# One kernel on one NeuronCore: the order of the query tiles in the prompt attention

## The chip, the cores and the metric

The kernel is one layer of a hybrid model, written in Bass for Trainium2. It runs as one program on one core of one chip. The metric is device time in microseconds (us), the median of several executions; the profile shows one execution of its own.

## The reference

A layer takes a prompt of 1024 tokens and a decode batch of 8 sequences with 4 tokens each. Half of the mixer is a gated linear recurrence (HGRN2), the other half is sparse attention with 8 query heads in 2 key-value groups (width 64), followed by an output projection and a convolutional feed-forward. The change touches the attention of the prompt alone. Its three branches, cut to the core:

```
o_cmp = softmax over compressed blocks of 16 tokens (63 of them), masked by position
o_slc = softmax over selected blocks of 64, at most 16: with 1024 prompt tokens all causal ones
o_win = softmax over the last 512 tokens
o = g[0] * o_cmp + g[1] * o_slc + g[2] * o_win      # g: sigmoid gates per token and head
```

With 1024 tokens there are only 16 blocks of 64, so that the selected branch is plain causal attention: query tile `qt` (128 queries) reads `qt + 1` key blocks of 128. The window branch reads at most 5 of them.

## The kernel before, in words

Six stages follow one another, with a barrier between them. `prompt_attention` is the fourth of them. It works through a list `units` written at L517 to L534: for each of the two key-value groups g one compressed unit C (all 8 query tiles at once), and then for every query tile qt one selected unit (SLC, S0 to S7 below) and one window unit (WND, W0 to W7). That makes 34 units. A unit Sq reads q + 1 key blocks, a unit Wq reads q + 1 of them up to 5.

Each unit has two halves of work:
- The **front**: for its 4 heads, TensorE computes scores (`scores`, L847 to L872) into one of two PSUM buffers `ps`, VectorE takes the row maximum (L781), ScalarE the exponential with its row sum (L694). A unit of up to 256 keys handles all 4 heads in one fill of a PSUM buffer, one of up to 512 keys two heads a fill, and a longer one needs 4 fills. A fill waits until the exponentials of the fill before last are done (L850 to L851). After the front VectorE computes four coefficients a row (L794, L795) and GpSimd scales the unit's probabilities by them (L651; L657 for unit C).
- The **back**, in groups of one key block each: TensorE transposes the scaled probabilities of 4 heads (`turn`, L890), ScalarE copies their high part (L708), VectorE forms the low part (L803), and TensorE multiplies both with the values (L910, L911) into the one accumulator `acc`. Even tiles have one more group in the window unit, for the compressed probabilities of two tiles (L704, L906, L907); odd ones use them again without a transpose (L914, L915). So the tiles must come in pairs 2k, 2k + 1.

After the last group of a window unit the tile's output leaves `acc` (L715 on ScalarE, L808 and L815 on VectorE), and SyncE stores it (L627).

All engines follow one list of steps. In step i, from -3 to 34, the back of unit i is interleaved with the front of unit i + 3:

```
    def merged(i):
        back = units[i].groups if 0 <= i < NU else 0
        front = units[i + AHEAD].fills if i + AHEAD < NU else 0
```

Steps -3 to 0 hold fronts alone (the fill of the pipeline), steps 31 to 34 backs alone (its drain). Steps 14 to 17 are the passage from group 0 to group 1, with unit C of group 1, whose front is long on TensorE. Every engine takes its instructions strictly in this order. In steps 1 to 3 ScalarE and VectorE also split the values and queries of group 1 (`second_high`, `second_low`; L676, L752, L680, L757).

SyncE has one queue: the stores of tile outputs in their order, between them the weights of the next stage (`w5a` at L623, `w5b` at L632), and from L633 on the first rows of the next stage (`o_front`, `x_front`).

Of the kernel before, what the change touches and what calls it, by code (L numbers as in the profile page):

```python
# [501 lines left out]
def prompt_attention(nc, io, keep, scratch, consts_sb):  # L502
# [3 lines left out]
    NQ = T // P  # L506
    NBK = NCP - 1
    CB = NCP
    CMP, SLC, WND = 0, 1, 2
# [4 lines left out]

    units = []
    n_fills = n_heads = n_groups = n_dense = 0
    for g in range(NG):  # L517
        for kind, qt in [(CMP, 0)] + [(kind, qt) for qt in range(NQ) for kind in (SLC, WND)]:
            u = Unit()
            u.n, u.g, u.kind, u.qt = len(units), g, kind, qt  # L520
            u.k0 = max(0, qt - 4) if kind == WND else 0
            u.blocks = [] if kind == CMP else list(range(u.k0, qt + 1))
            u.w = NQ * CB if kind == CMP else len(u.blocks) * P
            u.per = 4 if u.w <= 256 else 2 if u.w <= 512 else 1
            u.fills = R // u.per
            u.fill0, u.head0, u.group0, u.dense = n_fills, n_heads, n_groups, n_dense
            u.pair = kind == WND and qt % 2 == 0
            u.groups = len(u.blocks) + u.pair
            n_fills += u.fills
            n_groups += u.groups  # L530
            if kind != CMP:
                n_heads += R
                n_dense += 1
            units.append(u)  # L534
# [4 lines left out]
    pv_of_group, pv_before, n_pv = {}, {}, 0  # L539
# [19 lines left out]
    with ExitStack() as ctx:  # L559
# [30 lines left out]
        t_ready, h_ready, l_ready, pv_ready = (sem(n) for n in ("t_ready", "h_ready", "l_ready", "pv_ready"))  # L590
        half_ready, lower_ready, oT_ready = sem("half_ready"), sem("lower_ready"), sem("oT_ready")
        oT_out = [sem("oT_out0"), sem("oT_out1")]
# [19 lines left out]
        @block.sync  # L612
        def _(sp):
            for h in range(R):
                if h >= 2:
                    sp.wait_ge(qL_ready, h - 1)
                for d in range(2):
                    sp.dma_start(qs[h % 2][64 * d:64 * d + 64, :], scratch["q_T"][:, R + h, 0:T]).then_inc(q_in[h % 2], 16)
            sp.wait_ge(consts_sb["soft"]["p7_o_out"], 256)
            sp.wait_ge(kT_ready, 4)  # L620
            sp.wait_ge(vL_ready, 2)
            for k in range(4):
                sp.dma_start(keep["w5a"][:, k], io["w_out"][0, k * P:(k + 1) * P, :]).then_inc(consts_sb["soft"]["p5_w_in0"], 16)  # L623
            for a in range(NG * NQ):
                g, qt = a // NQ, a % NQ
                sp.wait_ge(oT_ready, 2 * (a + 1))
                sp.dma_start(scratch["o_T"][256 * g:256 * g + 256, qt * P:qt * P + P].rearrange("(k p) t -> p k t", p=P),  # L627
                             oT[a % 2][:]).then_inc(oT_out[a % 2], 16)
                if a == NQ:
                    sp.wait_ge(s_ready, units[NU // 2].fill0)  # L630
                    for k in range(4):
                        sp.dma_start(keep["w5b"][:, k], io["w_out"][0, (4 + k) * P:(5 + k) * P, :]).then_inc(consts_sb["soft"]["p5_w_in1"], 16)  # L632
                if a == NQ + 4:  # L633
                    sp.wait_ge(qL_ready, R)
                    for t in range(2):
                        sp.wait_ge(oT_out[t], 16 * (NQ // 2 + 1))
                        rows = slice(t * P, t * P + P)
                        done = consts_sb["soft"][f"p5_front_in{t}"]
                        sp.dma_start(keep["o_front"][:, t, 0:HGW], scratch["o_mix"][rows, 0:HGW]).then_inc(done, 16)
                        sp.dma_start(keep["o_front"][:, t, HGW:D].rearrange("p (k c) -> p k c", k=4),  # L640
                                     scratch["o_T"][:, rows].rearrange("(k p) c -> p k c", p=P)).then_inc(done, 16)
                        sp.dma_start(keep["x_front"][:, t], io["x_prompt"][0, rows, :]).then_inc(done, 16)
            for i in range(2):
                sp.wait_ge(oT_out[i], 16 * (NG * NQ // 2))
# [22 lines left out]
        def _(act):  # L667
# [29 lines left out]
            def high_of(u, k):  # L697
                G = u.group0 + k
                act.wait_ge(t_ready, G + 1)
                src = pt[G % 3][:].rearrange("p b c -> p (b c)")  # L700
                if u.pair and k == u.groups - 1:
                    if u.qt + u.g > 0:
                        act.wait_ge(pv_ready, pv_before[u.n - 2 if u.qt else u.n - 3])
                    nc.scalar.copy(PcH[:], src).then_inc(h_ready, 1)  # L704
                else:
                    if G >= 3:
                        act.wait_ge(pv_ready, pv_of_group[G - 3])
                    nc.scalar.copy(PTH[:, G % 3, :], src).then_inc(h_ready, 1)  # L708

            def upper_half(u):  # L710
                a = u.g * NQ + u.qt
                act.wait_ge(pv_ready, pv_before[u.n])
                if a >= 1:
                    act.wait_ge(oT_ready, 2 * a)
                nc.scalar.copy(half[:], acc[64:128, :]).then_inc(half_ready, 1)  # L715
# [25 lines left out]
        def _(dve):  # L741
# [61 lines left out]
                nc.vector.tensor_tensor(lo, src, hi.bitcast(F32), ALU.subtract).then_inc(l_ready, 1)  # L803

            def both_halves(u):
                a = u.g * NQ + u.qt
                dve.wait_ge(pv_ready, pv_before[u.n])
                nc.vector.tensor_copy(lower[:], acc[0:64, :]).then_inc(lower_ready, 1)  # L808
                dve.wait_ge(half_ready, a + 1)
                dve.wait_ge(lower_ready, a + 1)  # L810
                if a >= 2:
                    dve.wait_ge(oT_out[a % 2], 16 * (a // 2))
                for odd in range(2):
                    at = lambda x: x.rearrange("p (k o c) -> p k o c", k=2, o=2)[:, :, odd]
                    nc.vector.tensor_tensor(oT[a % 2][64 * odd:64 * odd + 64], at(lower[:]), at(half[:]), ALU.add).then_inc(oT_ready, 1)  # L815
# [22 lines left out]
        def _(pe):  # L838
# [53 lines left out]

            def values(u, k):
                G = u.group0 + k
                a = u.g * NQ + u.qt
                out = acc[:]
                pe.wait_ge(l_ready, G + 1)
                if u.kind == SLC and k == 0:
# [19 lines left out]
            for i in range(-AHEAD, NU + 1):  # L918
# [5 lines left out]
                for what, k in order:  # L924
# [5 lines left out]
                    else:  # L930
                        u = units[i + AHEAD]
# [2130 lines left out]
```

## Time and profile before

| | us |
|---|---|
| median of 3 runs | 2410.34 (2406.26 to 2414.07) |
| the profiled execution, its own time | 2406.49 |
| span of the profile | 2404.70 |
| from the first scores of the prompt attention (1171.28) to the store of its last tile (1472.16) | 300.88 |

The span is what the trace covers, from the first to the last instruction; the execution's own time is 1.79 us longer. All times below are from the start of the span.

### The profile page before, as it was taken

Reading aid. Unit: us, or ns where it says so; the run is one execution under the profiler, and the core shown is the slowest. Engines: PE = TensorE matmul, PEld = TensorE weight load, DVE = VectorE, ACT = ScalarE, POOL = GpSimd, SP = SyncE. Lnnn points to the kernel's source line nnn. Section 1 sums busy time; section 2 is a strip of 40 time slices with the busy share of each in tenths; the row PEclk is TensorE's granted clock in tenths of the full one; section 3 lists DMA queues with packets and bytes.
Section 4 is the critical chain, followed back from the end, with each engine's and each line's share of the span. In section 5 each row is a group of like instructions: output and inputs, shape, how many; then the busy total and the mean of one; then the engine's idle time right before and its main releaser. Section 6 shows DMA issues by size and latency. Waiting matters only on the chain. (4 is left out here: it accounts for less than half of the span.)

```text
span 2404.7 us, 39963 instructions
## 1 busy us (share of the span) xinstructions
PE 2256.3 (94%) x15806; PEld 2032.7 (85%) x15806; DVE 1307.0 (54%) x2975; ACT 945.3 (39%) x1910; POOL 513.0 (21%) x874
## 2 busy tenths in 40 slices
PE   6999999999999999869889898989999999999998
PEld 5999987877778777648767676869999999999998
DVE  5124137767767768743487786543333334355556
ACT  4114124555545544422275675212222222144444
POOL 0001004333324332200187683100000000011110
PEclk9999999999999999879699999989999999999999
DMA  4215726645446544297120112311111111122223
GB/s 122 68 53 188 279 100 214 219 161 182 167 151 217 172 155 133 52 284 229 36 62 5 44 43 72 109 52 49 44 44 52 44 44 44 52 84 80 81 72 119
DMA packets 213557, 263.10 MB, mean 109 GB/s; under 512 B 32658, under 2 KB 180370, under 8 KB 204018
## 3 DMA queue, kind: packets, MB, share of 16 engines
q1 hardware_dynamic: 195240, 159.71, 22.0%
q0 software_dynamic: 18160, 101.27, 12.1%
q8 instruction: 102, 1.67, 0.3%
q14 instruction: 55, 0.45, 0.1%
HBM read 202.76 MB, written 65.05 MB: 111 GB/s over the span
## 5 line engine op out<-in xcount | busy, mean ns | idle before, releaser
L1549 PE MATMUL f<-hH,wH 128*128 128x352 f32 x1056 | 341.4, 323 | 5.2 <-DVE wL L1422 5.2
L1549 PE MATMUL f<-hL,wH 128*128 128x352 f32 x1056 | 339.1, 321 | 0.0
L1549 PE MATMUL f<-hH,wL 128*128 128x352 f32 x1056 | 338.7, 321 | 0.0
L2527 ACT CAST a_XTH<-cpt 64x256 fp32r<-64x256 f32 (+1 forms) x576 | 200.9, 349 | 146.4 <-PE cpt L2734 135.8
L2643 DVE TENSOR_TENSOR a_XTL<-cpt,a_XTH 64x256 fp32r<-64x256 f32 (+1 forms) x576 | 230.3, 400 | 29.8 <-ACT a_XTH L2527 21.5
L1564 PE MATMUL f<-wdH,aH 128*128 128x256 f32 (+1 forms) x792 | 222.1, 285 | 8.7 <-DVE aL L1475 4.8
L1564 PE MATMUL f<-wdL,aH 128*128 128x256 f32 (+1 forms) x792 | 220.1, 284 | 0.0
L2749 PE MATMUL cph<-a_XTH,w1H 128*128 128x512 f32 x512 | 216.4, 423 | 0.0
L2749 PE MATMUL cph<-a_XTH,w1L 128*128 128x512 f32 x512 | 204.1, 399 | 0.0
L2749 PE MATMUL cph<-a_XTL,w1H 128*128 128x512 f32 x512 | 204.1, 399 | 0.0
L1549 PEld LDWEIGHTS f<-hH,wH 128*128 128x128 f32 x1056 | 198.6, 188 | 5.3 <-DVE wL L1422 5.3
L1564 PE MATMUL f<-wdH,aL 128*128 128x256 f32 x704 | 200.3, 285 | 0.0
L1549 PEld LDWEIGHTS f<-hL,wH 128*128 128x128 f32 x1056 | 198.9, 188 | 0.0
L1549 PEld LDWEIGHTS f<-hH,wL 128*128 128x128 f32 x1056 | 198.5, 188 | 0.0
L1422 DVE TENSOR_TENSOR wL<-raw,wH 128x1024 fp32r<-128x1024 f32 x44 | 53.8, 1225 | 225.1 <-ACT wH L1325 222.6
L1475 DVE TENSOR_TENSOR aL<-a_aT,aH 128x1408 fp32r<-128x1408 f32 x64 | 104.0, 1624 | 103.8 <-ACT aH L1363 103.5
L1564 PEld LDWEIGHTS f<-wdH,aH 128*128 128x128 f32 (+1 forms) x792 | 148.2, 187 | 11.0 <-DVE aL L1475 5.5
L1363 ACT CAST aH<-a_aT 128x1408 fp32r<-128x1408 f32 (+1 forms) x72 | 91.4, 1269 | 147.3 <-PE f L1564 147.3
L1564 PEld LDWEIGHTS f<-wdL,aH 128*128 128x128 f32 (+1 forms) x792 | 145.9, 184 | 0.0
L1564 PEld LDWEIGHTS f<-wdH,aL 128*128 128x128 f32 x704 | 136.3, 194 | 0.0
L486 PE MATMUL pj<-wH,xL 128*128 128x256 f32 (+2 forms) x464 | 130.9, 282 | 0.0
L486 PE MATMUL pj<-wH,xH 128*128 128x256 f32 (+2 forms) x464 | 130.8, 282 | 0.0
(486 smaller groups left out, 5358.4 us busy)
## 6 DMA issues: line engine op xcount, KB each, us to landing
raw<-in_w_in POOLq DMA_DIRECT2D x12, 1024.0 KB, 6.1
a_V<-v_s SPq DMA_DIRECT2D x6, 2048.0 KB, 12.1
v_s<-X SPq DMA_DIRECT2D x22, 512.0 KB, 6.2
raw<-in_w_gate SPq DMA_DIRECT2D x22, 512.0 KB, 3.9
raw<-in_w_val SPq DMA_DIRECT2D x22, 512.0 KB, 3.9
wraw<-in_w_down SPq DMA_DIRECT2D x44, 256.0 KB, 4.0
z_tok<-stage SPq DMA_DIRECT2D x48, 128.0 KB, 5.0
a_akq<-hq SPq DMA_DIRECT2D x32, 192.0 KB, 5.3
```

The lines of the kernel that those rows point to most:

```text
L486: last = nc.tensor.matmul(bank[u % 8][0:r, 0:nw], xp[:, k, a * P:a * P + r], wp[:, j % 2, k, 0:nw], **flags)
L1363: nc.scalar.copy(aH[:, h, :, 0:r], aT[:, NFH * h:NFH * h + NFH, t * P:t * P + r]).then_inc(aH_ready, 1)
L1422: nc.vector.tensor_tensor(wL[:, a], raw[:, a], wH[:, a].bitcast(F32), ALU.subtract).then_inc(wL_ready, 1)
L1475: nc.vector.tensor_tensor(dst, aT[:, NFH * h:NFH * h + NFH, t * P:t * P + r], aH[:, h, :, 0:r].bitcast(F32), ALU.subtract).then_inc(aL_rea ...
L1549: last = nc.tensor.matmul(bank[3 * a + n][:, 0:w], wp[:, a, k, :], hp[:, k, c0:c0 + w], start=(k + part == 0), stop=(k == KD - 1 and part ...
L1564: last = nc.tensor.matmul(bank[t % 3][0:rows, 0:QW], ap[:, h, j, 0:rows], wp[:, f, :], start=first, stop=final)
L2527: nc.scalar.copy(turned(XTH, u, s, k, g, a), split(bank(at, k)[:], u, k, g, a)).then_inc(h_ready, 1)
L2643: last = nc.vector.tensor_tensor(turned(XTL, u, s, k, g, a), split(bank(at, k)[:], u, k, g, a), hi.bitcast(F32), ALU.subtract)
L2749: last = nc.tensor.matmul(out[:, :, 0:n], w[:, s, k, q, m * P:(m + 1) * P], x[:, s % 2, k, :, q:q + n], **flags)
```

## The change

The query tiles of both groups are taken in the order 6 7 0 1 4 5 2 3 in place of 0 to 7. Buffers, semaphores and accumulations that counted by the tile number now count by its place in the order (`u.at`). SyncE stores the tiles in the new order, and starts the loads of `o_front` and `x_front`, which need tiles 0 and 1 of both groups, after the fourteenth of the 16 stores, one store later than before.

```diff
+    ORDER = [6, 7, 0, 1, 4, 5, 2, 3]
     for g in range(NG):
-        for kind, qt in [(CMP, 0)] + [(kind, qt) for qt in range(NQ) for kind in (SLC, WND)]:
+        for kind, qt in [(CMP, 0)] + [(kind, qt) for qt in ORDER for kind in (SLC, WND)]:
             u = Unit()
+            u.at = 0 if kind == CMP else ORDER.index(qt)
...
-                g, qt = a // NQ, a % NQ
+                g, qt = a // NQ, ORDER[a % NQ]
...
-                if a == NQ + 4:
+                if a == NQ + 5:
                     sp.wait_ge(qL_ready, R)
                     for t in range(2):
-                        sp.wait_ge(oT_out[t], 16 * (NQ // 2 + 1))
+                        sp.wait_ge(oT_out[t], 16 * (NQ // 2 + 2))
...
-                    if u.qt + u.g > 0:
-                        act.wait_ge(pv_ready, pv_before[u.n - 2 if u.qt else u.n - 3])
+                    if u.at + u.g > 0:
+                        act.wait_ge(pv_ready, pv_before[u.n - 2 if u.at else u.n - 3])
...
-                a = u.g * NQ + u.qt
+                a = u.g * NQ + u.at
```

(The last replacement stands at three places: `upper_half`, `both_halves` and `values`.)

What this does to the engines is seen first on GpSimd, from the scaling of unit C of group 0 on, for the first four tiles. Before, rows of `a_Prs` (selected units) and `a_Prw` (window units) widen from 128 columns:

```order
L657 TENSOR_TENSOR a_Pc<-a_Pc,a_cfc 128x2048
L651 TENSOR_SCALAR a_Prs<-a_Prs,a_cf 128x128 x4
L651 TENSOR_SCALAR a_Prw<-a_Prw,a_cf 128x128 x4
L651 TENSOR_SCALAR a_Prs<-a_Prs,a_cf 128x256 x4
L651 TENSOR_SCALAR a_Prw<-a_Prw,a_cf 128x256 x4
L651 TENSOR_SCALAR a_Prs<-a_Prs,a_cf 128x384 x4
L651 TENSOR_SCALAR a_Prw<-a_Prw,a_cf 128x384 x4
```

Now, at the same place (line numbers in the changed kernel are two higher):

```order
L659 TENSOR_TENSOR a_Pc<-a_Pc,a_cfc 128x2048
L653 TENSOR_SCALAR a_Prs<-a_Prs,a_cf 128x896 x4
L653 TENSOR_SCALAR a_Prw<-a_Prw,a_cf 128x640 x4
L653 TENSOR_SCALAR a_Prs<-a_Prs,a_cf 128x1024 x4
L653 TENSOR_SCALAR a_Prw<-a_Prw,a_cf 128x640 x4
L653 TENSOR_SCALAR a_Prs<-a_Prs,a_cf 128x128 x4
L653 TENSOR_SCALAR a_Prw<-a_Prw,a_cf 128x128 x4
L653 TENSOR_SCALAR a_Prs<-a_Prs,a_cf 128x256 x4
```

The four widest units of a group stand first, the four narrowest right behind them. VectorE at the fill of the pipeline (steps -2 to 0), from the coefficients of unit C on, before:

```order
L781 TENSOR_REDUCE a_nm<-s 128x4
L794 RECIPROCAL a_den<-a_den 128x4
L795 TENSOR_TENSOR a_cf<-a_den,gates 128x4
L781 TENSOR_REDUCE a_nm<-s 128x4
L794 RECIPROCAL a_den<-a_den 128x4
L795 TENSOR_TENSOR a_cf<-a_den,gates 128x4
L781 TENSOR_REDUCE a_nm<-s 128x2
```

and now:

```order
L783 TENSOR_REDUCE a_nm<-s 128x1 x4
L796 RECIPROCAL a_den<-a_den 128x4
L797 TENSOR_TENSOR a_cf<-a_den,gates 128x4
L783 TENSOR_REDUCE a_nm<-s 128x1 x4
L796 RECIPROCAL a_den<-a_den 128x4
L797 TENSOR_TENSOR a_cf<-a_den,gates 128x4
L783 TENSOR_REDUCE a_nm<-s 128x1 x4
```

Each front that took one fill and one maximum over all four heads now takes four fills and four maxima, before the first transpose of the back can follow. At the drain, VectorE's last rows before:

```order
L803 TENSOR_TENSOR a_PTL<-pt,a_PTH 128x512 x2
L808 COPY a_lower<-acc 64x512
L815 TENSOR_TENSOR a_oT<-a_lower,a_half 64x256 x2
L803 TENSOR_TENSOR a_PTL<-pt,a_PTH 128x512 x11
L808 COPY a_lower<-acc 64x512
L815 TENSOR_TENSOR a_oT<-a_lower,a_half 64x256 x2
```

and now:

```order
L805 TENSOR_TENSOR a_PTL<-pt,a_PTH 128x512 x2
L810 COPY a_lower<-acc 64x512
L817 TENSOR_TENSOR a_oT<-a_lower,a_half 64x256 x2
L805 TENSOR_TENSOR a_PTL<-pt,a_PTH 128x512 x6
L810 COPY a_lower<-acc 64x512
L817 TENSOR_TENSOR a_oT<-a_lower,a_half 64x256 x2
```

The last tile (S3, W3) has 8 groups where it had 13 (S7, W7); with W2 in place of W6 in step 31 the drain has 12 groups in place of 19. No instruction of the stage is added or removed.

## Rows read from the trace of the kernel before

**Rows 1.** the page of the profile, its first line.

```profile
span 2404.7 us, 39963 instructions
```

**Rows 2.** stretches of the prompt attention, all engines; columns in the first line.

```profile
core 0: us, PE busy (x) PEld busy (x) DVE busy (x) ACT busy (x) POOL busy (x), PEclk, DMA share, GB/s
1171.28:1186.64 15.36, 15.36 (x70) 14.97 (x69) 4.01 (x5) 1.78 (x3) 0.00 (x0) 0.50 0.14 35
1186.64:1196.04 9.40, 8.29 (x38) 7.81 (x38) 8.46 (x11) 3.96 (x17) 2.11 (x1) 0.50 0.00 0
1196.04:1305.12 109.08, 94.37 (x545) 79.46 (x546) 92.80 (x144) 78.27 (x173) 94.59 (x61) 0.95 0.12 37
1305.12:1346.88 41.76, 35.05 (x225) 30.07 (x224) 27.41 (x41) 17.61 (x42) 15.15 (x10) 0.92 0.02 4
1346.88:1448.33 101.45, 90.20 (x545) 76.31 (x545) 87.08 (x140) 73.55 (x167) 90.47 (x56) 0.98 0.15 51
1448.33:1472.14 23.81, 20.22 (x121) 15.55 (x119) 17.92 (x30) 13.29 (x24) 9.20 (x5) 1.00 0.02 6
```

**Rows 3.** timeline of the stage's end; start, duration, engine, line, operation, idle before.

```profile
1470.06 0.40 PE L915 MATMUL acc<-a_PcL,VC 128*128 128x512 f32 x1
...
1472.16 0.36 SPq L627 DMA_DIRECT2D o_T<-a_oT  x1
```

**Rows 4.** timeline of TensorE: one fill (1406.27), two transposes a group apart.

```profile
1406.27 0.40 PE L866 MATMUL s<-a_KTb,a_Qb 128*128 128x512 f32 x1
...
1407.19 0.60 PE L890 MATMUL pt<-ident,a_Prw 128*128 128x128 f32 x4
...
1408.09 0.60 PE L890 MATMUL pt<-ident,a_Prw 128*128 128x128 f32 x4
```

**Rows 5.** groups by shape, VectorE, 1220 to 1472: count, busy, mean ns, idle, releaser.

```profile
L803 DVE TENSOR_TENSOR a_PTL<-pt,a_PTH 128x512 fp32r<-128x512 f32 x128 | 87.5, 688 | 28.9 <-ACT a_PTH L708 26.8
L781 DVE TENSOR_REDUCE a_nm<-s 128x1 f32<-128x640 f32 x40 | 32.8, 820 | 1.3 <-PE s L871 1.0
...
L808 DVE COPY a_lower<-acc 64x512 f32<-64x512 f32 x15 | 10.1, 674 | 1.3 <-PE acc L915 1.3
...
L781 DVE TENSOR_REDUCE a_nm<-s 128x1 f32<-128x896 f32 x8 | 8.7, 1083 | 0.2
...
L787 DVE TENSOR_REDUCE a_denc<-a_Pc 128x32 f32<-128x2048 f32 x1 | 2.3, 2274 | 0.0
```

**Rows 6.** groups by shape, ScalarE, 1220 to 1472.

```profile
L694 ACT ACTIVATE a_Prw<-s,a_nm 128x640 f32<-128x640 f32 x32 | 25.5, 798 | 21.7 <-DVE a_nm L781 21.6
L694 ACT ACTIVATION_READ_ACCUMULATOR a_Prs<-s,a_nm 128x1 f32 x52 | 10.3, 198 | 0.0
...
L694 ACT ACTIVATE a_Prs<-s,a_nm 128x896 f32<-128x896 f32 x8 | 8.1, 1010 | 3.8 <-DVE a_nm L781 3.6
```

**Rows 7.** list of waits, 1171 to 1472: us in total, times, longest.

```profile
ACT a_Prw L694 <- DVE a_nm L781: 31.9, 19, 2.8
DVE a_PTL L803 <- ACT a_PTH L708: 27.0, 51, 1.2
...
PE acc L910 <- DVE a_lower L808: 11.1, 12, 3.5
```

**Rows 8.** timeline of GpSimd: scaling of C, S6, S7 in group 0.

```profile
1193.93 3.62 POOL L657 TENSOR_TENSOR a_Pc<-a_Pc,a_cfc 128x2048 f32<-128x2048 f32 x1 [161.54 <-DVE a_cfc L790]
...
1275.21 10.04 POOL L651 TENSOR_SCALAR a_Prs<-a_Prs,a_cf 128x896 f32<-128x896 f32 x4 [2.11 <-DVE a_cf L795]
...
1295.39 11.43 POOL L651 TENSOR_SCALAR a_Prs<-a_Prs,a_cf 128x1024 f32<-128x1024 f32 x4 [1.32 <-DVE a_cf L795]
```

**Rows 9.** timeline of VectorE: the two additions of a tile's output.

```profile
1229.26 0.87 DVE L815 TENSOR_TENSOR a_oT<-a_lower,a_half 64x256 f32<-64x256 f32 x2
...
1329.52 2.55 DVE L815 TENSOR_TENSOR a_oT<-a_lower,a_half 64x256 f32<-64x256 f32 x2
```

**Rows 10.** DMA issues, 1380 to 1500: count, KB each, median us to landing.

```profile
x_front<-in_x_prompt SPq DMA_DIRECT2D x2, 512.0 KB, 5.6
```

More of the change, by code:

```diff
@@ L805, in both_halves @@
             def both_halves(u):
-                a = u.g * NQ + u.qt
+                a = u.g * NQ + u.at
                 dve.wait_ge(pv_ready, pv_before[u.n])
@@ L894, in values @@
                 G = u.group0 + k
-                a = u.g * NQ + u.qt
+                a = u.g * NQ + u.at
                 out = acc[:]
```

## Prediction

> **What bounds the kernel now.** I read the page first [rows 1]: the span is 2404.70 us, and the profiled execution took 2406.49. Then I cut the prompt attention into stretches [rows 2]. Their borders are the first TensorE instruction of a step, found by counting TensorE's rows in the timeline against the program's order: steps -2 to 0 are 1186.64 to 1196.04, steps 1 to 13 end at 1305.12, 14 to 17 at 1346.88, 18 to 30 at 1448.33, and the drain ends with the store of the last tile at 1472.16 [rows 3]. The reader is to see two things there. First, no engine is full: in steps 1 to 13 TensorE is busy for 94.4 of 109.1 us, VectorE for 92.8, GpSimd for 94.6; in 18 to 30 for 90.2, 87.1 and 90.5 of 101.5. Second, the three are alike, so whichever has most to do in a step sets that step, and the rest is handover. The list of waits says the same [rows 7]: ScalarE waits 31.9 us for maxima, VectorE 27.0 for high parts, TensorE 11.1 for the accumulator to be emptied. So the order can change only how long the pipeline fills and drains, and how evenly the steps load the engines.
>
> **Term 1, the fill: +18 us.** Before, steps -2 to 0 take 9.4 us [rows 2], because S0, W0 and S1 need one fill each. Now S6, W6 and S7 need four each, twelve in all. A fill of S6 takes TensorE 0.92 us at the full clock (1406.27 to 1407.19) [rows 4], up to twice that while the granted clock is 0.50, as it is in this stretch [rows 2]; then VectorE takes 1.08 [rows 5], ScalarE 1.01 and 0.20 [rows 6], and three handovers cost about 0.1 to 0.2 each. With two PSUM buffers two fills share one such chain of about 3.9 us (TensorE's part taken between the two clocks), so one costs 1.95; for W6 (VectorE 0.82, ScalarE 0.80) it is 1.55. VectorE also has unit C's coefficients in between: 2.3 for the sum [rows 5] and about 0.8 for three short ones. I walked it: S6's first maximum ends near 1190.8, C's coefficients near 1194.1, S6's last exponential near 1200.7, W6's near 1207.7, S7's third at 1213.9. Step 1 begins with a fill that needs this last one: 1214 in place of 1196, which is +18. From below: GpSimd starts S6 when the coefficients are there, 1200 at best, and needs 10.04 us [rows 8], and no transpose of S6 comes before 1210: +14. From above: twelve fills at 2.4 us (half clock throughout) and 3.1 for C: 1219, +23.
>
> A rule weighed here: the Trainium skill, "TensorE: Matmul & The Clock Gate", Part 1, says that the reduced clock is the default and sustained activity of the array releases it. This trace agrees as far as it goes: the clock is 0.50 over C's narrow matmuls and the small fills behind them, and 0.95 in the mean of steps 1 to 13. By that rule the wider matmuls of S6 and W6 would bring the full clock some microseconds earlier; the sum would have +15 here in place of +18.
>
> **Term 2, the two long stretches: -8 us.** I added up each step's work for both orders. VectorE: 0.69 us a group (L803), for a maximum 0.16 us and 1.03 ns a column (the line through 0.82 at 640 and 1.08 at 896) [rows 5], 0.35 for the two short operations on a unit's coefficients, 1.95 for a tile's output (0.67 for L808 [rows 5], and 1.28 for L815 between 0.87 and 2.55 [rows 9]). TensorE: 0.90 a group (1407.19 to 1408.09), 0.92 a fill of 896 columns, others in proportion [rows 4]. Step 13 before, for one, holds 7 groups of S6, four maxima of W7, coefficients and an output: VectorE 4.8 + 3.3 + 0.35 + 1.95 = 10.4, TensorE 9.8. The larger load, summed over the steps, is 98.7 for steps 1 to 13 and 92.6 for 18 to 30; the trace has 109.08 and 101.45 [rows 2], so a step costs 1.10 times its larger load. In the new order the sums are 95.0 and 91.3: times 1.10, 204.9 in place of 210.5, -5.6. They fall because work left these steps: the fronts of S6, W6 and S7 stand in the fill and the passage, and more of the backs, seven groups, come into them. VectorE's loads alone go from 187.7 to 177.5; if it paced everything, at 1.12 as before, that would be -11.4. Small steps behind long ones let the queues even out in part, so I take -8, between the two. The small tiles in the middle are not free: W7's last group is multiplied only when TensorE reaches W0's first transposes, VectorE holds its next maximum until that output is out, and a fill of S4 waits some 3 us; this is in the 1.10.
>
> **Term 3, the passage between the groups: +2 us.** Steps 14 to 17 take 41.76 us [rows 2]. They lose 7 groups of S7, W7 and W6 in the sum (19 before, 12 now), and gain the twelve fills of S6, W6 and S7 for three: TensorE's load goes from 28.4 to 30.3 and VectorE's from 29.3 to 34.3. Both engines have room there (35.1 and 27.4 busy of 41.8), and a walk like that of term 1 gave 41.8 again. I take TensorE's difference, +2; the bounds are 0 and +5.
>
> **Term 4, the drain: -6.3 us.** Steps 31 to 34 hold 12 groups for 19, with nothing beside them: seven by 0.90 [rows 4]. At the 1.1 us that a group costs with its waits it is 7.7, and 5 if the last tile's output, now behind shorter steps, is waited for.
>
> **What costs nothing.** The loads of `o_front` and `x_front` start one store later, and so nearer the end: after the output of tile 5, near step 30, some 16 us before the last store. Six issues of half a microsecond and 5.6 us to land [rows 10] make 9; if that cover were gone, the last store would wait for them by up to 9 us. GpSimd needs 10.0, 7.5, 11.4 and 7.5 us for S6, W6, S7 and W7 [rows 8] (W at the same rate a column), one behind the other until about 1238; TensorE wants W7 some 30 us after step 1 starts, 1244, so it is not late, with 6 us to spare. VectorE and ScalarE's split of group 1's values and queries, 6 us on VectorE, now falls on full steps; its load is in the sums.
>
> **The sum.** 18 - 8 + 2 - 6.3 = +5.7. On the profiled execution's own 2406.49 that is 2412.2. The median of the runs shown is 2410.34, 3.85 above this execution, so the forecast for the median is 2416.0. A measurement of this kernel can tell about 0.3% (7.2 us) from no change: below 2403.1 is faster, above 2417.6 slower.
>
> **The rivals.**
> - Evening out pays for the long fill. VectorE paces all (-11.4), the passage shortens by 2 because the fills of S6 cover C's long front, the drain gives 7.7, the fill costs only 14: -7.1, and 2403.2; with a passage 3 shorter still, 2400. For it: VectorE's ratio of measured to load is nearly the same in both stretches, 1.126 and 1.118. Against it: TensorE has the larger load in half of the new steps. Chance 0.18.
> - The tile outputs get slower. L815 took 0.87 us a pair at 1229.26 and 2.55 at 1329.52 [rows 9]; the second is while GpSimd scales, the first too, but with shorter instructions. If the wide units up front bring ten of the 16 pairs from 0.9 to 2.5, VectorE has 16 us more, half of it on the path: 2424. It decides from 1.6 us on, where the forecast crosses 2417.6. Against it: GpSimd's busy time is the same 211.5 us (the sum of its column [rows 2]) in both orders. Chance 0.16. The Trainium skill, "SBUF — State Buffer", section "SBUF: two separate sides", states a mechanism: a VectorE operation with two SBUF inputs and a GpSimd operation exclude each other on a shared port pair, for a whole instruction. The two rows of L815 agree with it; by it a pair could wait as long as one scaling of 1024 columns.
> - The order does not matter: what is saved in the middle and the drain is the fill and no more, 2410. Chance 0.08.
> - The forecast, 2410 to 2422 by the bounds of its terms: chance 0.58, of it 0.34 below 2417.6, 0.23 above and 0.01 below 2403.1.
>
> **How the numbers follow.** Faster: 0.17 of the first rival and 0.01: 0.18. Same: 0.34, 0.01, 0.03 and 0.08: 0.46. Slower: 0.23 and 0.13: 0.36. The range reaches from 2403 (the first rival's sum) to 2425 (the second's), with a tenth outside on either side.
>
> **What would show it.** TensorE's first group (step 1) near 1214; steps 1 to 13 in 103 to 106 us and 18 to 30 in 97 to 101; the passage in 42 to 45; from the last maximum to the last store 17 to 18 us for 24. The page's VectorE and GpSimd busy times within 5 us of before. The prediction is wrong if the granted clock is full right behind C and the fill takes 14 or less, if the long stretches fall by 12 or more together, if L815's pairs take 2 us or more, or if TensorE waits for GpSimd at the first transposes of S6 or S7.

## The result and the profile after

The new order is slower. Its median is 2438.86 us (2432.53 to 2439.96) against 2410.52 for the kernel before in the same comparison, a ratio of 1.0113 with a 95% interval of 1.0095 to 1.0132. The forecast was 2416, with a range to 2425.

The page of the changed kernel and its stretches of the prompt attention, cut at the same steps as [rows 2] (the columns are the same; unit C's front, steps -2 to 0, 1 to 13, 14 to 17, 18 to 30, 31 to the last store):

```profile
span 2436.6 us, 39964 instructions
...
1170.73:1183.01 12.28, 12.28 (x71) 12.01 (x69) 4.00 (x5) 1.78 (x3) 0.00 (x0) 0.64 0.19 43
1183.01:1211.00 27.99, 21.54 (x66) 16.42 (x66) 18.25 (x23) 12.44 (x23) 17.30 (x7) 0.61 0.00 0
1211.00:1324.92 113.92, 94.74 (x558) 79.91 (x559) 83.18 (x139) 73.76 (x172) 81.44 (x54) 0.94 0.11 34
1324.92:1377.94 53.02, 47.60 (x212) 41.46 (x210) 32.49 (x46) 21.93 (x42) 27.07 (x14) 0.69 0.02 6
1377.94:1484.86 106.92, 93.47 (x559) 79.37 (x560) 78.91 (x136) 69.59 (x167) 78.31 (x53) 0.95 0.08 28
1484.86:1503.85 18.99, 13.92 (x79) 10.15 (x77) 14.15 (x23) 9.34 (x18) 8.98 (x6) 1.00 0.39 125
```

Set against [rows 2], the differences are: unit C -3.1, fill +18.6, steps 1 to 13 +4.8, passage +11.3, steps 18 to 30 +5.5, drain -4.8: +32.3, and the span grew by 31.9. The fill and the drain came as forecast. Two lines did not. The long stretches grew, though VectorE has 9.6 and 8.2 us less to do in them (83.18 for 92.80, 78.91 for 87.08); TensorE's busy time did not fall with it (94.74 for 94.37, 93.47 for 90.20). And the passage runs at a granted clock of 0.69 in place of 0.92.

The list of waits, 1171 to 1504 (us in total, times, longest), answers to [rows 7]:

```profile
ACT a_PTH L710 <- PE pt L892: 60.8, 55, 7.7
...
DVE a_PTL L805 <- ACT a_PTH L710: 43.1, 60, 1.6
...
DVE a_nm L783 <- PE s L873: 26.2, 29, 2.3
...
PE acc L912 <- DVE a_lower L810: 19.4, 10, 4.2
```

and one line of the kernel before, 1171 to 1472, beside them:

```profile
DVE a_nm L781 <- PE s L871: 5.0, 8, 2.7
```

VectorE waits more for TensorE's scores (26.2 us for 5.0, the long fill included) and for ScalarE's high parts (43.1 for 27.0), and TensorE's wait for an emptied accumulator has gone from 11.1 to 19.4 us. In the two long stretches alone TensorE waits 15.2 us for the accumulator where it was 6.3, and 7.3 for low parts where it was 1.5; for probabilities it waits 11.0 where it was 18.5. These waits and its longer busy time (+3.6) add up to 10.8 us, and the two stretches grew by 10.3. The tile outputs, the second rival of the prediction, are the group L817 by shape, over the whole of the stage (count, busy, mean ns):

```profile
L817 DVE TENSOR_TENSOR a_oT<-a_lower,a_half 64x256 f32<-64x256 f32 x32 | 15.7, 490 | 2.0
```

A pair takes 0.98 us in the mean; the forecast of that rival needed 1.6 or more for ten of the pairs. It is not the cause.

### The profile page after: what moved, and what is told of

Its sections match the earlier page's. It is cut to its first block and busy times, and to the rows that moved or that the text cites. A ratio compares the mean times of both kernels' runs of the same rounds, so it can differ in the third digit from the quotient of the medians.

```text
span 2436.6 us, 39964 instructions
## 1 busy us (share of the span) xinstructions
PE 2272.9 (93%) x15806; PEld 2043.8 (84%) x15806; DVE 1303.9 (54%) x2975; ACT 946.8 (39%) x1910; POOL 512.5 (21%) x874
```

## The experiments

In all of them the order of tiles is the one line `ORDER = [6, 7, 0, 1, 4, 5, 2, 3]`, written for each group apart where they differ. With it moves the place of the loads of `o_front` and `x_front`: behind the thirteenth store in the kernel before, the fourteenth in the new order and wherever group 1 starts with 6 7 0 1, the twelfth where tiles 0 and 1 come first in group 1, and the last one in 6 7 4 5 0 1 2 3. Times are medians with the ratio to the kernel before, measured beside it; stretches come from one profile each. "C, fill, 1-13, passage, 18-30, drain" are in us, the drain to TensorE's last matmul (22.1 before, 17.3 after). Nothing ahead of the stage is changed, yet it began anywhere from 1170.4 to 1181.5 us in these profiles; so stretches are compared, and not spans. The stretches of one kernel vary too: two more profiles of the new order, below, gave 116.6 and 113.4 us for steps 1 to 13 and 106.9 and 106.1 for 18 to 30.

| kernel | ratio (95%) | C | fill | 1-13 | passage | 18-30 | drain |
|---|---|---|---|---|---|---|---|
| before | 1 | 15.4 | 9.4 | 109.1 | 41.8 | 101.5 | 22.1 |
| new order | 1.0113 (1.0095-1.0132) | 12.3 | 28.0 | 113.9 | 53.0 | 106.9 | 17.3 |
| group 1 alone new | 1.0041 (1.0028-1.0053) | 9.3 | 9.4 | 109.2 | 53.7 | 105.6 | 17.1 |
| group 0 alone new | 1.0093 (1.0066-1.0120) | 15.4 | 27.8 | 115.7 | 36.3 | 101.4 | 22.1 |
| 6 7 4 5 0 1 2 3 | 1.0083 (1.0062-1.0105) | 12.3 | 28.0 | 109.1 | 42.8 | 101.3 | 16.9 |
| 0 1 6 7 2 3 4 5 | 1.0059 (1.0038-1.0081) | 12.3 | 9.4 | 118.7 | 42.0 | 109.4 | 19.3 |
| 0 1 2 3 6 7 4 5 | 0.9989 (0.9979-0.9998) | 12.3 | 9.4 | 109.8 | 40.0 | 103.4 | 19.3 |
| 6 7 0 1 2 3 4 5 | 1.0080 (1.0063-1.0097) | 15.4 | 27.9 | 107.0 | 52.8 | 97.4 | 19.3 |

**Each half of the change alone.**

```
-    ORDER = [6, 7, 0, 1, 4, 5, 2, 3]
+    ORDER = [[0, 1, 2, 3, 4, 5, 6, 7], [6, 7, 0, 1, 4, 5, 2, 3]]   # group 1 alone; group 0 alone: exchanged
```

> Tiles 0 to 7 in group 0, the order 6 7 0 1 4 5 2 3 in group 1 alone. The trace of the changed kernel shows four parts: the fill (+15.5 us, counted from unit C's first scores), the long stretch of group 0 (+4.8), the passage (+11.3), the long stretch of group 1 (+5.5) and the drain (-4.8). Theory A: most of the passage's loss is the granted clock, which fell to 0.50 as the short steps of group 0's last tiles ran into unit C's narrow matmuls. With S7 and W7 in front of C, as before, the clock should stay up and the passage cost 42 to 45 us. Then this kernel has +2, +5.5 and -4.8: about +3 us, 2413, same as before within the measurement. Theory B: the passage is long because twelve fills of S6, W6 and S7 follow C, whatever stands ahead of it. Then it takes 50 us or more and the kernel is at +12, 2422.

> The new order in group 0 alone, tiles 0 to 7 in group 1. Theory A: fill +15.5, first long stretch +4.8, and the passage still has C's front at the lower clock behind short steps, +6 to +8, with short fronts S0, W0 and S1 behind it: +26 to +28 us in all, about 2438. The second stretch and the drain are as before. Theory B: the passage is short again, as three one-fill fronts follow C, 42 us: +20 us in all, 2431.

Measured: 2418.92 and 2432.07. The passage of group 1 alone took 53.7 at a granted clock of 0.94, so it is long without a fall of the clock when 19 groups stand beside twelve fills. Group 0 alone carries the fill (+18.4) and a longer first stretch (+6.6), and gets back 5.5 in a passage with 12 groups of backs and short fronts; group 1 alone carries a passage with 19 groups and twelve fills (+11.9), a second stretch longer by 4.2, and the shorter drain (-5.0). So both stretches get longer in the new order, whatever the other group does: no accident of one place.

**Other orders of long and short.**

> Order 6 7 4 5 0 1 2 3 in both groups: tiles 0 and 1 stand behind 4 and 5 and not behind 6 and 7; fill and drain are those of the changed kernel. Theory A (one-fill fronts beside long backs and short steps behind long ones cost the stretches): the fronts of S0, W0 and S1 meet backs of 6, 6 and 5 groups in place of 6, 8 and 5, and no four-fill front meets a one-group back any more (S4 stood beside W0); the stretches get 3 to 5 us shorter each, 2431 in all. Theory C (only the sum of the work of a step counts, and the clock): no change against the changed kernel, 2439.

> Order 0 1 6 7 2 3 4 5 in both groups: the fill is that of the kernel before (9.4 us for steps -2 to 0), the passage has the full clock ahead of C (tiles 4 and 5) and short fronts behind it, the drain has 16 groups for 19. By theory A what is left is the cost of taking long and short tiles by turns in the stretches, +3 to +5 us each, less 2.7 for the drain: +3 to +8 us, 2414 to 2418. If turns of long and short cost nothing themselves, it is at -3 us, 2407.

Measured: 2428.36 and 2425.09. Stepping down in pairs has the same instructions in the stretches as the new order but for their order, and takes 109.1 and 101.3: nothing more than before, and nothing less either, though the loads of its steps are smaller (95.0 for 98.7 and 91.3 for 92.6 by the prediction's prices). It is still slower by the fill; its front loads went out after the last store, and what stands behind that store took 6.2 us more than in the kernel before, which takes part of what it gains. The order 0 1 6 7 2 3 4 5 has no long fill, and yet 118.7 and 109.4; 0 1 2 3 6 7 4 5, further below, has the same instructions in these steps as well, and takes 109.8 and 103.4, the second at the same granted clock of 0.97. So it is not the amount of work but the neighbours.

**Unit C's mask product four times over**, to give TensorE wide matmuls among the 64-column ones (work added, nothing taken away), in the new and in the old order; and **the new order unchanged**, a second time.

```
-                        nc.tensor.matmul(s[:, c0:c0 + 512], eye[:], cmask[:], start=True, stop=True)
+                        for _ in range(4):
+                            nc.tensor.matmul(s[:, c0:c0 + 512], eye[:], cmask[:], start=True, stop=True)
```

> The changed kernel with the 512-column mask matmul that opens each head of unit C issued four times in place of once (the result is the same, since each one starts the accumulation anew). Twelve more matmuls of about 0.21 us for each C, 2.6 us at the full clock. What is open is why the passage took 53.0 us in the changed kernel and 42.8 in the order 6 7 4 5 0 1 2 3, where steps 14 to 17 hold the same instructions: the granted clock was 0.50 for 24 us over C's front in the one and full in the other. Theory A (the clock, and C's narrow matmuls cannot bring it back): with wide matmuls among them C's front of group 1 runs at the full clock, and the passage takes 45 to 47 us, the fill's C 10 to 12: -5 to -8 us, 2431. Theory B (the 53 us have another cause): +3 to +5 us, 2443.

> The same edit in the kernel before. C's front of group 0 took 15.36 us there at clock 0.50, and C's of group 1 had the full clock but for one drop. Theory A: the first C gets the full clock on the way and takes 11 to 13 us for 15.4, the small fills behind it are faster by 1 to 2, and group 1's C pays 2.6 for nothing: -2 to +1 us, 2409. Theory B (the clock does not follow what C's front does): C takes 20 us at half clock and the kernel is at +8.

> The changed kernel once more, for a second profile and in the same job as its variants. In the order 6 7 0 1 4 5 2 3 for group 0 alone the instructions up to the passage were the same, and yet the clock did not fall over C's front. If the fall is a matter of how the execution lies in time, this profile may have it or not, with the passage at 53 or at 43 us; if it belongs to the order, it falls again. The time stays 2438.9 within 4 us either way.

Measured: 2437.51, ratio 1.0118 (1.0097 to 1.0139); 2406.43, 0.9991 (0.9980 to 1.0002), which is no difference that can be told; and 2443.23, 1.0134 (1.0111 to 1.0157). With the dense C the passage took 45.5 in both orders, at a granted clock of 0.96 in the new one and 0.92 in the old; the unchanged kernel showed 53.0 again. So most of the passage's +11.3 goes with the clock. But the dense C is worth little in the median, so this profile alone did not settle the clock.

**Two fills in place of one for narrow tiles.**

```
-            u.per = 4 if u.w <= 256 else 2 if u.w <= 512 else 1
+            u.per = 2 if u.w <= 512 else 1
```

> The changed kernel with the fronts of tiles 0 and 1 (windows of up to 256 keys) in two fills of two heads in place of one fill of four. Steps 2 to 4 and 19 to 21 are where long backs of 6, 8 and 5 groups meet the one-fill fronts of S0, W0 and S1; TensorE waits there 2.4, 4.2 and 3.2 us for low parts and for the emptied accumulator, because ScalarE puts four heads' exponentials (1.4 to 1.9 us) and VectorE a maximum over four heads between two groups. Theory D (these bursts make the stretches longer): half a burst each time, steps 1 to 4 and 18 to 22 shorter by 2 to 3 us each, 2434. Theory E (it is the short steps behind them, 5 to 7 and 22 to 24, where a four-fill front has only one or two groups beside it): no gain, and 0 to +2 us for eight more fills.

Measured: 2436.51, 1.0115 (1.0091 to 1.0140), stretches of 116.8 and 104.4. Steps 18 to 22 took 37.2 us, 1.5 less than the new order's same steps at the full clock (38.7), which is a little under the 2 to 3 us expected of the bursts; the median does not show it.

**The fill of a short front held back** to the place where TensorE waits for the accumulator. Where a long SLC unit stands beside a front of one or two fills, the first of them is issued ahead of the first group, and nothing is left to multiply between the last tile's end and the third group of this one.

```
             for k in range(back):
-            while f < front and f * back <= k * front:
+            held = back > 2 and front < 4 and units[i].kind == SLC and k < 2
+            while f < front and f * back <= k * front and not held:
```

> The new order, but in the step of a slc unit with more than two groups the fills of a front that has one or two of them are not issued ahead of the first group: they stand just ahead of the third, where TensorE would otherwise wait for the accumulator to be emptied (S7 beside W0, S5 beside W2, S2 beside W3; in the passage S3 beside C has four). Theory A (the stretches got longer because a long slc unit stands beside a front of one or two fills, so nothing covers the wait for the accumulator): TensorE's waits for a_lower at these steps (4.2, 2.5, 1.7 in steps 3, 11, 13 and 2.1, 2.5, 1.7 in steps 20, 28, 30) fall to under 1 each, steps 1 to 13 take 109 to 111 in place of 113.9 to 116.6, steps 18 to 30 take 102 to 104 in place of 106.9; the median is 6 to 10 below the new order's, near 2431. Theory B (the handover between the four engines sets these steps, and the wait only moves to another semaphore): the waits for PTL or for probabilities grow by what a_lower loses, the stretches stay within 1.5 of the new order's, and the median is within 3 of it.

> The same, and unit C's mask product issued four times as in the dense C run. If the clock's fall over group 1's C is the other large part of the loss, the passage takes 45 to 46 here with the granted clock above 0.9, against 53 with the clock at half, and the median is 5 to 8 below that of the hold alone; by theory A for the stretches as well it lands near 2425, by theory B near 2433.

Measured: 2431.18, 1.0098 (1.0073 to 1.0123); with the dense C 2434.47, 1.0123 (1.0102 to 1.0145). TensorE's waits, 1183 to 1490, first the new order (third profile), then with the fill held:

```profile
PE acc L912 <- DVE a_lower L810: 19.6, 10, 4.2
...
PE acc L912 <- DVE a_PTL L805: 10.5, 11, 2.2
```

```profile
PE acc L913 <- DVE a_PTL L806: 16.8, 17, 2.7
...
PE acc L913 <- DVE a_lower L811: 6.3, 6, 3.2
```

Of 13.3 us of waits for the accumulator taken away, 6.3 came back as waits for low parts. The second stretch fell from 106.1 to 103.65 (102.4 with the dense C, against 105.5). The first took 115.9, inside the 113.4 to 116.6 of the unchanged order; with the dense C it fell from 114.9 to 112.1. Both theories hold in part: the wait is real, and half of it is the handover, which comes back. The medians of the new order and of this one lie too near each other to rank them.

**Fills held back in the ascending order** (the same line without `front < 4`). Beside every long SLC unit all fills that are due before the third group, up to three of them, then stand together just ahead of it.

> The ascending order with the first fill of every front held back to just ahead of the third group in the step of a slc unit with more than two groups. Theory A: the waits for a_lower there are small already (3.1 us in each stretch, 3.5 in step 15), so at most 5 us could be gained and the delayed fill costs some of it: 2404 to 2412. Theory B: each held fill delays maximum and probabilities of the next unit by two groups, 1.5 us in about half of the steps: 2414 or more.

Measured: 2427.45, 1.0094 (1.0077 to 1.0111); I had put 2404 to 2412 for the theory of the accumulator and 2414 or more for the handover, and the second came. Steps 1 to 13 and 18 to 30:

```profile
1194.67:1311.09 116.42, 99.12 (x545) 83.13 (x545) 90.64 (x144) 77.79 (x173) 93.69 (x61) 0.91 0.11 35
1356.02:1461.35 105.33, 90.30 (x546) 76.18 (x545) 84.67 (x140) 73.12 (x167) 89.36 (x56) 0.98 0.15 49
```

No instruction is added and the tiles stand as before, yet the stretches take 7.3 and 3.9 us more, the second at the same granted clock as before (0.98; the first at 0.91 for 0.95). In the second TensorE's wait for the accumulator fell from 3.2 to 0.3 us, and its wait for window units' probabilities rose from 4.2 to 11.8. That is the strongest evidence that the stretches are set by where fills stand between groups, as much as by how many there are.

**One jump up, one down, never onto a short front.**

> Order 0 1 2 3 6 7 4 5 in both groups: it jumps up once (3 to 6) and down once (7 to 4), but no long slc unit stands beside a front of fewer than four fills. Theory A: steps 1 to 13 and 18 to 30 take 1.10 times their larger loads of 100.1 and 94.0, 110 and 103, the fill is 9.4, the passage 42, the drain 19.3: 2408 to 2412, as before. Rival (any jump in length costs, as in 0 1 6 7 2 3 4 5): stretches of 115 and 108, and 2420 or more.

Measured: 2402.70, 0.9989 (0.9979 to 0.9998). The fill, steps 1 to 13, passage, 18 to 30 and drain:

```profile
1182.63:1192.02 9.39, 8.28 (x37) 7.80 (x38) 8.45 (x11) 3.95 (x17) 2.10 (x1) 0.50 0.00 0
1192.02:1301.87 109.85, 96.75 (x557) 81.21 (x557) 93.58 (x147) 79.33 (x175) 94.75 (x61) 0.94 0.12 37
1301.87:1341.83 39.96, 33.30 (x214) 28.58 (x212) 25.04 (x38) 16.32 (x40) 14.63 (x10) 0.91 0.02 4
1341.83:1445.19 103.36, 93.62 (x558) 79.21 (x558) 87.61 (x143) 74.61 (x169) 90.64 (x56) 0.97 0.15 50
1445.19:1464.44 19.25, 17.87 (x109) 13.95 (x107) 14.04 (x24) 11.51 (x21) 8.69 (x5) 1.00 0.03 8
```

The stretches are 1.10 times their larger loads (100.1 and 94.0), as expected: a jump in length costs nothing here, where no long SLC unit has a front of fewer than four fills beside it. It has the lowest ratio of the study, 0.02 to 0.21% ahead of the kernel before, at the edge of what can be told (the dense C in the old order, 0.9991, can't be told from it); its passage and drain are shorter by 1.8 and 2.9, its stretches longer by 2.7.

The wait itself, TensorE's first values of tile 7 in group 1. First the new order (third profile), where the front beside S7 is W0 with one fill, then this order, where it is W4 with four, then the new order with the fill held, where these values follow without a wait and those of the fourth group wait for their low part instead:

```profile
1392.98 0.62 PE L912 MATMUL acc<-a_PTH,a_V2b 128*128 128x512 f32 x1 [2.16 <-DVE a_lower L810]
```

```profile
1418.97 0.47 PE L912 MATMUL acc<-a_PTH,a_V2b 128*128 128x512 f32 x1 [1.04 <-DVE a_lower L810]
```

```profile
1402.38 0.47 PE L913 MATMUL acc<-a_PTH,a_V2b 128*128 128x512 f32 x1
...
1406.71 0.50 PE L913 MATMUL acc<-a_PTH,a_V2b 128*128 128x512 f32 x1 [0.98 <-DVE a_PTL L806]
```

**The short tiles followed by 2 and 3 in place of 4 and 5.**

> Order 6 7 0 1 2 3 4 5 in both groups: the long tiles still stand right ahead of the short ones, but the short ones are followed by tiles 2 and 3, whose fronts have one to two fills for the four of 4 and 5. If the short backs beside four-fill fronts are the rest of the excess, steps 18 to 21 take 36.4 as with the dense C run and steps 22 to 30 as their like in the ascending order, about 59: 95 in all, 8 over the larger loads of 86.9. If the long backs beside short fronts are, the excess stays at 12 to 14 and the stretch takes 99 to 101. The passage has 17 groups beside twelve fills, near 50; drain 19.3; fill 28. In sum 2416 to 2420 by the first, 2424 to 2428 by the second.

Measured: 2428.03, 1.0080 (1.0063 to 1.0097). Steps 18 to 21 and 22 to 30:

```profile
1374.01:1412.04 38.03, 33.56 (x212) 28.41 (x213) 26.95 (x47) 24.19 (x62) 26.62 (x18) 0.96 0.19 63
1412.04:1471.44 59.40, 52.95 (x317) 44.79 (x316) 50.97 (x85) 43.27 (x103) 51.42 (x36) 0.97 0.07 21
```

Steps 22 to 30 came out at 59.4, as expected if short backs beside four-fill fronts cost something: 3.4 over their larger loads of 56.0, where the new order's same steps take 68.1, 7.8 over 60.3. TensorE's waits in these steps, first the new order (third profile), then this one:

```profile
PE acc L912 <- DVE a_lower L810: 4.4, 3, 2.5
PE s L868 <- ACT a_Prs L696: 3.1, 4, 2.3
PE s L868 <- ACT a_Prw L696: 1.7, 3, 0.8
```

```profile
PE s L868 <- ACT a_Prs L696: 2.8, 2, 2.0
PE s L868 <- ACT a_Prw L696: 2.2, 3, 1.2
PE acc L912 <- DVE a_lower L810: 1.3, 3, 0.8
```

The fills wait as long for probabilities without the four-fill fronts of 4 and 5 beside short backs (5.0 us) as with them (4.8). What differs by 3.1 is the wait for the accumulator, at tiles 5 and 2. Steps 18 to 21 took 38.0 for 36.4: still 7 over their 30.9, as in the new order (38.1), where the same four backs beside long fronts in 0 1 2 3 6 7 4 5 take 41.3, only 3.2 over 38.1. So long backs beside fronts of one or two fills cost some 4 us a stretch in steps 18 to 21 and 3 more in 22 to 30; that short backs beside four fills cost anything of their own is not shown. The median was at the upper case all the same: steps 1 to 13 took 107.0, and the passage 52.8, of which the clock was at half for 17.

**Is it the order that lowers the clock?** One profile each.

> Group 0 in the new order, group 1 ascending, once more. If the order of what stands ahead of group 1's C decides the clock, it falls here as in the new order, and step 14 takes some 22 us; if the single execution decides, it can go either way. In the first profile of this kernel it did not fall.

> The new order once more. Step 14 took 22.0 us at half clock in both profiles so far. If the kernel's timing decides, again 22; if the execution does, perhaps 14 to 18 with the clock kept.

> The dense C in the new order once more: the passage took 45.5 with the clock kept, but 50.4 with 10 us of half clock where the fills were held. If the wide mask products keep the clock, 45 to 46 again; if not, it may fall here too.

Measured: single executions of 2425.85, 2428.10 and 2431.45, passages of 36.3, 44.4 and 45.5, the granted clock over group 1's C 0.87, 0.87 and 1.00. The changed kernel's step 14 (group 1's C) and step 15 first as profiled at the start:

```profile
1324.92:1346.94 22.02, 22.02 (x94) 20.64 (x92) 9.62 (x14) 4.67 (x9) 8.77 (x6) 0.50 0.03 7
1346.94:1360.22 13.28, 10.25 (x46) 8.78 (x44) 11.78 (x16) 7.15 (x14) 3.62 (x1) 0.76 0.04 10
```

and the same kernel in the third profile, step 14 and then the four stretches (fill, 1 to 13, passage, 18 to 30):

```profile
1324.68:1337.92 13.24, 13.24 (x94) 12.45 (x92) 8.24 (x13) 4.15 (x8) 8.47 (x6) 0.87 0.04 11
...
1183.29:1211.28 27.99, 21.60 (x66) 16.49 (x66) 18.26 (x23) 12.45 (x23) 17.30 (x7) 0.60 0.00 0
1211.28:1324.68 113.40, 93.97 (x559) 79.07 (x559) 83.05 (x139) 73.68 (x172) 81.23 (x54) 0.94 0.11 34
1324.68:1369.10 44.42, 36.59 (x212) 30.96 (x210) 33.43 (x46) 21.73 (x42) 27.23 (x14) 0.92 0.02 7
1369.10:1475.22 106.12, 92.08 (x558) 77.48 (x559) 78.84 (x136) 69.39 (x167) 78.71 (x53) 0.97 0.08 28
```

The same 94 matmuls, with TensorE busy without a gap both times, take 22.0 us at 0.50 and 13.2 at 0.87. One kernel does both. Two of its three profiles had the fall; the dense C kept the clock in two profiles, and the dense C with the fill held lost it for 10 us. So the fall belongs to the execution; whether the order makes it likelier is open. Of the nine executions of the new order the two fastest, 2428.10 and 2432.53, have the highest mean clock of the whole program, 0.966; the others have 0.956 to 0.963. So the median above most likely holds the fall. No other order showed a fall as long, but most were profiled once.

**The clock inside the long stretches.** It falls there too, for single steps. Step 20 of the new order (S7 beside W0) in the third profile, and in that of group 1 alone:

```profile
1387.10:1399.64 12.54, 10.38 (x62) 8.82 (x60) 8.50 (x15) 6.58 (x18) 6.72 (x7) 0.86 0.35 121
```

```profile
1381.09:1392.02 10.93, 8.77 (x61) 7.54 (x60) 8.56 (x15) 6.57 (x18) 6.76 (x7) 1.00 0.25 79
```

Such a fall costs 1.6 us, so a difference of 2 us between two single profiles can be one of them. It is not the main cause of the long stretches. A step at the full clock takes the same time within 0.1 us in every profile that has the same units in it, and each of the steps 18 to 30 was seen at the full clock in both orders (the dense C and the two halves of the change have the same steps there). These add up to 103.04 us in the new order and 99.38 in the ascending one, so +3.7 of the +4.7 to +5.5 is there without any fall of the clock.

## Why the prediction was wrong

**Term 1, the fill, was right:** +18 forecast, +18.6 measured, step 1 at 1211.0. The forecast had 1214, but unit C's own front was 3.1 shorter, a part of the clock that I had taken as given: it took 9.3 to 15.4 us in the profiles of this study. The estimate by chains of two fills came out: 27.4 us forecast for steps -2 to 0, 28.0 measured. GpSimd was indeed not late:

```profile
1197.32 10.05 POOL L653 TENSOR_SCALAR a_Prs<-a_Prs,a_cf 128x896 f32<-128x896 f32 x4 [3.41 <-DVE a_cf L797]
1207.35 7.46 POOL L653 TENSOR_SCALAR a_Prw<-a_Prw,a_cf 128x640 f32<-128x640 f32 x4
1214.79 12.22 POOL L653 TENSOR_SCALAR a_Prs<-a_Prs,a_cf 128x1024 f32<-128x1024 f32 x4
```

S6 is scaled at 1207.4 and its first transposes start at 1212.0; no wait for scaled probabilities is among TensorE's.

**Term 2, the long stretches, is the step that failed: -8 forecast, +10.3 measured** (+4.8 and +5.5; +4.3 and +4.7 with the clock kept). The work did leave these steps: VectorE's busy time fell by 17.8 in the two together, more than the 10.2 of the forecast's loads. What failed is "a step costs 1.10 times its larger load". That factor was read from an order in which every back of n groups has a front of nearly its own length beside it. For steps 18 to 30 the runs gave, of the larger load: ascending 1.10, up then down 1.10, stepping down 1.11, short tiles rising behind 6 and 7 1.12, the new order 1.16 (1.13 at the full clock, where ascending is 1.07). For steps 1 to 13 it was 1.10, 1.10, 1.15 for stepping down, and 1.19 to 1.23 for the new order. Where a long back stands beside a front of one or two fills, TensorE runs out of fills between the groups and waits for the accumulator or for low parts: 22.5 us in the two stretches for 7.8. Where a back of one or two groups stands beside four fills, it waits for the previous fill's probabilities. I had seen the second ("a fill of S4 waits some 3 us") and booked it into the 1.10, and over both stretches these waits fell, 11.0 for 18.5. The first I did not see, and so left at what it costs in the ascending order. The hold and the orders show that the first costs; how much of the excess is this wait, and how much the handover that comes back when it is taken away, is open. None of the prediction's signs of being wrong came: it had none for stretches that grow.

**Term 3, the passage, was right in mechanism, +2 forecast and +2.7 measured with the clock kept.** In the execution shown first it was +11.3; the other 8.6 are the half clock over unit C, which no term held. The forecast's sum with the measured sizes of the terms and the clock kept is 18.6 + 9.0 + 2.7 - 4.8 = 25.5 in place of 5.7; with unit C's -3.1 it is 22.4, and the third profile's span was 21.6 above before. The half clock's 8.6 and 1.3 more in the stretches make it 32.3 for the first, whose span grew by 31.9. So with the clock kept this kernel would still have missed: of the 19.8 us between 5.7 and 25.5 term 2 has 17.0.

**Term 4, the drain:** -6.3 forecast, -4.8 measured, just under its lower bound of 5. TensorE waits 2.1 us for low parts in it, before 0.7.

**What costs nothing** held. The front loads were not waited for (the store of the last tile follows its output by 0.02 us), and the remainder of the program is the same within half a microsecond.

**The rivals.** Evening out did not pay: VectorE's loads fell and nothing followed. The tile outputs took less than before (0.98 us a pair, 490 ns each). "The order does not matter" is refuted by the new order's own median, and by orders with the same instructions in the stretches that differ by 6 to 9 us there. The rival that I lacked is that mixing long and short pairs can make neighbours worse; my forecast took the even loads of a step for an even flow within it.

## What to carry to other kernels

A factor of measured time over load belongs to the neighbours that it was measured with: before it is put to a new order, list for each step what stands beside what, and look for steps in which one stream has nothing to put into the other's waits. In a software pipeline with unlike tiles give a long unit a front with enough fills beside it, take short ones first for a short fill, and if the end is long, a middle pair last may be worth a try (0.1% here, at the edge of what can be told). And before a difference of 10 us is put down to an order, profile one kernel more than once: here one profile in three told another story about the clock.

## What was not expected of the hardware

The granted clock stayed at 0.50 for 22 us in which TensorE was busy throughout. It had fallen just before: TensorE had waited 1.7 us for the accumulator, and the second matmul behind that wait is already slow. In the third profile the same wait stands at the same place, and the clock stays up behind it. First profile, then third:

```profile
1324.18 0.52 PE L912 MATMUL acc<-a_PTH,V2a 128*128 128x512 f32 x1 [1.71 <-DVE a_lower L810]
1324.50 0.63 PE L913 MATMUL acc<-a_PTL,V2a 128*128 128x512 f32 x1
```

```profile
1324.14 0.47 PE L912 MATMUL acc<-a_PTH,V2a 128*128 128x512 f32 x1 [1.71 <-DVE a_lower L810]
1324.45 0.39 PE L913 MATMUL acc<-a_PTL,V2a 128*128 128x512 f32 x1
```

The 64-column matmuls of unit C stand 0.21 us apart in the first profile, in the third profile 0.11. A part of unit C in the first profile:

```profile
1337.92 0.40 PE L860 MATMUL s<-KCH,a_Qb 128*128 128x64 f32 x1
1338.13 0.40 PE L860 MATMUL s<-KCL,a_Qb 128*128 128x64 f32 x1
```

and in the third, behind the mask product:

```profile
1332.70 0.28 PE L860 MATMUL s<-KCH,a_Qb 128*128 128x64 f32 x1
1332.81 0.28 PE L860 MATMUL s<-KCL,a_Qb 128*128 128x64 f32 x1
```

The 0.50 is the 1.2 GHz level; the transposes and values between C's fills were slowed with it (1.11 us for four transposes at 1343.46, against 0.60 in [rows 4]). The Trainium skill, "TensorE: Matmul & The Clock Gate", Part 1, says that sustained activity releases the full clock; by that one would expect the full clock to come back within these 22 us without a gap, and in the first profile it did not. The same part says that the ramp at a kernel's start differs from run to run of one kernel; here the three profiles of the changed kernel differ in the middle of it. What in the array's work decides it, no run here shows.
